# A three-stage transformer kernel on one core: five modulation groups of each feed-forward loop get buffers of their own, with their column sums behind the loop

## The reference, cut to what matters

```python
def ada(cvec, w, b):
    return jnp.split(jax.nn.silu(cvec) @ w + b, 6, axis=-1)

def swiglu(h, w1, w3, w2):
    return (jax.nn.silu(h @ w1) * (h @ w3)) @ w2

x = x + g1 * out_l
x = x + g2 * swiglu(rmsnorm(x, norm2_g[i]) * (1 + sc2) + sh2, ffn_w1[i], ffn_w3[i], ffn_w2[i])
```

## Time and profile before

| what | value |
|---|---|
| median of three runs | 1949.84 us (1944.81 to 1951.23) |
| profiled execution, its own time | 1940.54 us |
| its span, first to last instruction | 1938.7 us |
| busy: TensorE, weight loads, DVE, ACT, POOL | 88%, 56%, 46%, 22%, 19% |
| 40 to 263 us: norm, projections, attention, first residual | TensorE 197.1 of 223 us, clock 0.91 |
| 263 to 479 us: feed-forward loop, layer 0 | TensorE 206.1, DVE 193.7, POOL 103.6 of 216 us, clock 0.97 |
| 479 to 551 us: Fourier mixer | TensorE 62.3 of 72 us |
| 551 to 766 us: feed-forward loop, layer 1 | TensorE 204.3, DVE 194.1, POOL 105.1 of 215 us, clock 0.98 |
| 766 to 940 us: second block's mixer, routing | TensorE 127.4 of 174 us, clock 0.81 |
| 940 to 1938 us: experts | TensorE 882.6 of 998 us, loads at 393 GB/s, DMA share 0.95 |

### The profile page before, as it was taken

The page is one execution under the profiler, slowest core; times in us unless marked ns, Lnnn a source line. Parts: engine busy times, 40 slices in busy tenths (PEclk is TensorE's granted clock), DMA queues, the critical chain, the costliest instruction groups (busy, mean ns, idle before and its releaser), DMA issues.

```text
span 1938.7 us, 24538 instructions
## 1 busy us (share of the span) xinstructions
PE 1704.7 (88%) x9524; PEld 1084.9 (56%) x9524; DVE 888.1 (46%) x1218; ACT 435.8 (22%) x669; POOL 369.1 (19%) x119
## 2 busy tenths in 40 slices
PE   6989889999889998877898798999698999598995
PEld 2863679999689998756543242433242444143432
DVE  5766578998369998675422121221120222021113
ACT  3325543443344443452100000000000000000001
POOL 1631034543334553552000000000000000000000
PEclk9998989999999999887799899999899999899998
DMA  9533367886358886342769999999999999999992
GB/s 356 195 101 117 117 228 272 283 276 206 112 204 276 286 284 211 119 141 78 298 276 421 421 421 421 421 416 421 421 422 421 421 407 421 421 421 421 422 420 107
DMA packets 100463, 586.59 MB, mean 303 GB/s; under 512 B 12208, under 2 KB 13488, under 8 KB 44880
## 3 DMA queue, kind: packets, MB, share of 16 engines
q1 hardware_dynamic: 100368, 585.32, 77.7%
HBM read 584.22 MB, written 1.05 MB: 302 GB/s over the span
## 4 chain that ended last, share of the span: by engine, by line
PE 54%; DMA 19%; DVE 15%; issue 8%; ACT 2%; SPq 1%; DVEq 0%; ACTq 0%
PE psum L990 17%; DMA mraw<-gu_dram 10%; PE psum L1006 10%; DVE acc L1542 5%; DMA araw<-ada_dram 3%; PE psum L966 3%; DMA mraw<-dn_dram 2%; PE psum L566 2%; DMA mlast<-dn_dram 2%; PE psum L567 2%; PE psum L568 2%; PE psum L1019 2%; DVE acc L1541 1%; SPq L378 1%; DVE wl L1814 1%
## 5 line engine op out<-in xcount | busy, mean ns | idle before, releaser
L990 PE MATMUL psum<-mraw,xsat 128*64 128x512 f32 (+2 forms) x1912 | 472.3, 647 | 66.7 <-DMA mraw<-gu_dram 52.6
L1478 POOL TENSOR_TENSOR wl<-raw,wh 128x1024 fp32r<-128x1024 f32 (+1 forms) x100 | 360.1, 3611 | 517.3 <-ACT wh L1106 295.2
L990 PEld LDWEIGHTS psum<-mraw,xsat 128*64 128x64 f32 (+2 forms) x1912 | 160.3, 145 | 353.2 <-issue 352.3
L1006 PE MATMUL psum<-mraw,xsat 128*64 128x512 f32 (+2 forms) x928 | 227.5, 620 | 27.0 <-DMA mlast<-dn_dram 18.9
L747 PE MATMUL psum<-ah,wh 128*128 128x256 f32 x704 | 203.5, 289 | 15.4 <-DVE al L1589 11.6
L748 PE MATMUL psum<-al,wh 128*128 128x256 f32 x704 | 201.4, 286 | 0.0
L749 PE MATMUL psum<-ah,wl 128*128 128x256 f32 x704 | 201.2, 286 | 0.0
L566 PE MATMUL psum<-ah,wh 128*128 128x256 f32 (+1 forms) x440 | 136.6, 311 | 35.0 <-DVE al L1589 11.3
L1006 PEld LDWEIGHTS psum<-mraw,xsat 128*64 128x64 f32 (+2 forms) x928 | 78.3, 141 | 154.6 <-issue 151.7
L747 PEld LDWEIGHTS psum<-ah,wh 128*128 128x128 f32 x704 | 137.2, 195 | 17.0 <-issue 12.0
L2107 DVE TENSOR_TENSOR oacc<-psum,oacc 128x512 f32<-128x512 f32 x64 | 41.2, 685 | 229.1 <-PE psum L1019 229.1
(11 more groups left out here) (341 smaller groups left out, 2457.2 us busy)
## 6 DMA issues: line engine op xcount, KB each, us to landing
mraw<-gu_dram SPq DMA_DIRECT2D x239, 1024.0 KB, 19.3
mraw<-dn_dram SPq DMA_DIRECT2D x116, 1024.0 KB, 24.9
araw<-ada_dram SPq DMA_DIRECT2D x128, 512.0 KB, 4.4
raw<-ffa_dram SPq DMA_DIRECT2D x44, 1024.0 KB, 7.3
raw<-blk_dram SPq DMA_DIRECT2D x56, 512.0 KB, 3.7
raw<-ffb_dram SPq DMA_DIRECT2D x44, 512.0 KB, 5.1
mlast<-gu_dram SPq DMA_DIRECT2D x17, 1024.0 KB, 20.9
mlast<-dn_dram SPq DMA_DIRECT2D x12, 1024.0 KB, 22.4
```

What stands on the lines that cost most here:

```text
L990: last = mm(ps[4 + n][a * w:(a + 1) * w, :], xs[:, k * P + a * w:k * P + (a + 1) * w], slots[slot][:, i * 2 * D + n * 512:i * 2 * D + (n + ...
L1006: last = mm(ps[n][a * w:(a + 1) * w, :], at[:, k * P + a * w:k * P + (a + 1) * w], slots[slot][:, i * D + n * 512:i * D + (n + 1) * 512], ...
L1478: sub = lambda o, a, b: nc.gpsimd.tensor_tensor(o, a, b.bitcast(F32), ALU.subtract)
```

## The change

`acc` stays for the groups outside the loops. Inside a loop each of the five groups has a buffer of its own in `accl` [128 x 5 x 1024] (it lies over `vdft`), addressed by a register that moves with the pass, so that nothing in the loop waits for column sums. The column step leaves the loop. Behind the loop TensorE makes the sums as rows (`loop_rows`): for each half of 512 columns five products with a 128 x 32 matrix of one column of ones, the first four into four strips of 32 rows, the fifth added to the first strip. ACT copies the rows to `lrow`, TensorE turns them into forty columns with eight products (`loop_columns`, behind the norm's sums), and DVE adds forty biases at once (`loop_mods`). DVE's bias of group 5 and 11 moves ahead of the loop. In `norm_split(4)` the gain now follows the reciprocal. POOL's clears wait for the last loop's column products, because `accl` and `lrow` share memory with what is cleared. Two constants are added to `con`, 69 columns in all: `strip` (128 x 64, zero but for column 32) and `pick5` (128 x 5, which picks rows 0, 32, 64, 96 and 1). The hunks of the two constants are left out:

```diff
@@ -188,7 +188,11 @@
...
         tabs = sb("tabs", [P, 2, 3, T], F32, base)
-        vdft = sb("vdft", [P, TT, 4, 2 * T], F32, base)
+        over = ExitStack()
+        vdft = sb("vdft", [P, TT, 4, 2 * T], F32, over)
+        over.close()
+        accl = sb("accl", [P, 5 * AG], F32, base)
+        lrow = sb("lrow", [P, AG], F32, base)
         base.close()
...
@@ -240,7 +244,7 @@
...
         ps = [psum[:, i, :] for i in range(8)]
-        ps45, ps67 = [psum[:, i:i + 2, :].rearrange("p a n -> p (a n)") for i in (4, 6)]
+        ps01, ps45, ps67 = [psum[:, i:i + 2, :].rearrange("p a n -> p (a n)") for i in (0, 4, 6)]
...
@@ -545,6 +549,25 @@
...
+            def loop_rows(l):
+                pe.wait_ge(s_ada, 8 * (9 + 6 * l))
+                for half in range(2):
+                    for i in range(5):
+                        a, one = 32 * (i % 4), _C["strip"] + (32 if i < 4 else 31)
+                        last = mm(ps[half][a:a + 32, :], con[:, one:one + 32],
+                                  accl[:, i * AG + half * 512:i * AG + (half + 1) * 512], start=(i < 4), stop=(i > 0),
+                                  skip_group_check=True)
+                last.then_inc(s_adp, 1)
+
+
+            def loop_columns(l):
+                pe.wait_ge(s_arow, 3 + l)
+                pe.wait_ge(s_mod, 6 + 6 * l)
+                for i in range(8):
+                    last = mm(ps[2][:, 5 * i:5 * i + 5], lrow[:, i * P:(i + 1) * P], C("pick5", 5), start=True, stop=True)
+                last.then_inc(s_acol, 5)
+
+
             def norm_sums(n):
...
@@ -769,21 +792,17 @@
...
                         gate_up(f0 + (2 + u), u)
-                        if u == 2:
-                            pe.wait_ge(s_ada, i * 8 + (8 * (5 + 6 * l)))
-                            pe.wait_ge(s_mod, i + (6 + 6 * l))
-                            for k in range(8):
-                                last = mm(ps[2][:, k:k + 1], acc[:, k * P:(k + 1) * P], ones[:, 0:1], start=True, stop=True)
-                            last.then_inc(s_acol, 1)
                         down(f0 + (1 + u), u + 1)
...
             ffn(0)
+            loop_rows(0)
...
             norm_sums(2)
+            loop_columns(0)
             pe.wait_ge(s_par, DFT_IN)
...
@@ -810,9 +829,11 @@
...
             ffn(1)
+            loop_rows(1)
...
             norm_sums(4)
+            loop_columns(1)
             for b in range(B_2, B_V2):
...
@@ -1118,6 +1139,10 @@
...
+            def loop_row(l):
+                act.wait_ge(s_adp, 9 + l)
+                A(lrow[:, :], ps01, ACT.Copy).then_inc(s_arow, 1)
+
             def norm_root(n, width=T):
...
@@ -1295,6 +1320,7 @@
...
             norm_squares(2, x_by_ffn(0))
+            loop_row(0)
             norm_root(2)
...
@@ -1319,6 +1345,7 @@
...
             norm_squares(4, x_by_ffn(1))
+            loop_row(1)
             act.wait_ge(s_fdn, 1 + 2 * NF)
...
@@ -1504,6 +1531,7 @@
...
             pool.wait_ge(s_fml, 2 * NF)
+            pool.wait_ge(s_acol, 17)
             nc.gpsimd.memset(rga[:, :, :], 0.0).then_inc(s_zero, 1)
...
@@ -1546,7 +1574,7 @@
...
                 if j == 0:
-                    dve.wait_ge(s_acol, g)
+                    dve.wait_ge(s_acol, {11: 6, 17: 12}.get(g, g))
                 else:
...
@@ -1563,6 +1591,14 @@
...
+            def loop_mods(l):
+                g = 6 + 6 * l
+                dve.wait_ge(s_acol, g + 5)
+                TTn(mod[:, 8 * g:8 * g + 40].rearrange("p (g i) -> p g i", i=8),
+                    ps[2][:, 0:40].rearrange("p (i g) -> p g i", g=5),
+                    vec[:, _V["ada_b"] + 8 * g:_V["ada_b"] + 8 * g + 40].rearrange("p (g i) -> p g i", i=8), ALU.add
+                    ).then_inc(s_mod, 5)
+
             def m_col(g, j):
...
@@ -1577,9 +1613,13 @@
...
             def norm_split(n, gain, g_shift, hl):
-                norm_gain(gain, g_shift)
+                if n != 4:
+                    norm_gain(gain, g_shift)
                 dve.wait_ge(s_rt, n + 1)
                 link(V_.reciprocal(rstd[:, 0:T], rt[:, 0:T]))
+                if n == 4:
+                    loop_mods(1)
+                    norm_gain(gain, g_shift)
                 for j in range(DJ + 2):
...
@@ -1606,6 +1646,8 @@
...
                             mod_ready(1)
+                        if n == 2:
+                            loop_mods(0)
                         norm_gain(gain, g_shift)
...
@@ -1813,32 +1855,25 @@
...
+                mod_ready(base_g - 1)
                 down_lo(0, 0)
...
                     loaded = dve.snap(i * 64 + 16 * (base_n // 2 - 7))
-                    col = dve.snap(i * 8 + 8 * (base_g - 1))
-                    cols = dve.snap(i + base_g)
+                    g0 = dve.snap(i * AG)
                     for u in range(4):
                         mul(f0 + u, u % 2)
-                        if u == 0:
-                            dve.wait_ge(s_acol, cols)
-                            TTn(mod[:, bass.ds(col, 8)], ps[2][:, 0:8], vec[:, bass.ds(col + _V["ada_b"], 8)], ALU.add
-                                ).then_inc(s_mod, 1)
                         for j in (2 * u, 2 * u + 1):
                             dve.wait_ge(s_araw[j % 2], loaded + 16 * (j // 2))
-                            if j == 0:
-                                dve.wait_ge(s_acol, cols)
-                            else:
+                            if j > 0:
                                 dve.wait_ge(s_ada, n0 + j)
-                            ada_step(acc[:, :], araw[:, j % 2, :], csil[:, j:j + 1] if l == 0 else V("c2", j), j
+                            ada_step(accl[:, bass.ds(g0, AG)], araw[:, j % 2, :], csil[:, j:j + 1] if l == 0 else V("c2", j), j
                                      ).then_inc(s_ada, 1)
...
                 mul(NF - 2, 0)
-                mod_ready(base_g + 4)
                 mul_lo(NF - 2, 0)
...
```

More of the change, by code:

```diff
@@ L116 @@
 for _name, _m in [("ident", 128), ("ones", 128), ("triu", 128), ("iota", 128), ("iota32", 32), ("pair8", 32), ("head8", 64),
-                  ("bcast8", 8 * QD), ("cos", T), ("sin", T), ("rot", ROPE), ("mask", 2 * P), ("ekey", NEXP), ("capkey", NEXP), ("capval", NEXP), ("erow", 1), ("first", 1), ("pick", 2)]:
+                  ("bcast8", 8 * QD), ("cos", T), ("sin", T), ("rot", ROPE), ("mask", 2 * P), ("ekey", NEXP), ("capkey", NEXP), ("capval", NEXP), ("erow", 1), ("first", 1), ("pick", 2), ("strip", 64), ("pick5", 5)]:
     _C[_name] = _n
@@ L2178, in constants @@
     put("bcast8", np.repeat(np.eye(HEADS), QD, axis=1))
+    put("strip", np.broadcast_to(np.arange(64) == 32, (P, 64)) * 1.0)
+    put("pick5", (r[:, None] == np.array([0, 32, 64, 96, 1])) * 1.0)
     put("pick", np.eye(32, 2)[r[:64] % 32])
```

## The result

Seven runs of the changed kernel gave a median of 1934.49 us (1927.47 to 1938.81), seven runs of the kernel before on the same chip 1944.81 us: ratio **0.9918, 95% interval [0.9896, 0.994]**. The forecast was 8.3 us less, 0.4%; the ratio says 0.8%. (The two medians lie 10.3 us apart, the averages of the same runs, 1947.6 and 1933.0, 14.6.) The direction and the next bound of the loops came as forecast; the size was about half of what the ratio says, for terms that the sum had too small or not at all. The profiled execution took 1928.56 us (span 1926.7), 12.0 less than that of before (1940.54).

The account below looks back on a forecast made before the run. TensorE's column step bounded the loops, with the load chain next at 36.8 us a pass. Loops -13.0, layer 0's tail +1.6, layer 1's +3.0 and constants +0.1 gave -8.3 from 1949.84: 1941.5 us, range 1930 to 1951.

Parts of the forecast that it names:

- The next bound: In the feed-forward loops, what limits a four-tile pass once the column step is gone: 36.8 us a pass, POOL first.
- the load chain: In the loops, wide load, ACT copy, POOL split, DVE accumulate, next wide load's issue: 18.5 us over two tiles.
- The chosen state: In the loops, POOL's split comes first and DVE's accumulate ends behind it, in all passes: 36.8 us a pass.
- The loops, -13.0: Both feed-forward loops: -4.9 and -3.5 us up to the fifth waits, -2.3 twice behind them; ends -32.0 and -7.4.
- Layer 0's tail, +1.6: Behind layer 0's loop: row sums of about 3.6 us put the reciprocal +1.3 later, the 40-column add +0.3.
- Layer 1's tail, +3.0: Behind layer 1's loop: POOL's clears delay its block splits and DVE's norm products; +3.0 us, ends 0.45 and 3.6.
- The start, +0.1: Constants' load: 69 more columns, 35 KB in one load, cost +0.1 us.
- The end, nothing: Expert stage behind the loops: a gain or loss ahead of it passes through in full, with no term of its own.
- TensorE's floor: Rival for the loops: only TensorE remains as bound, passes of 34.56 us, 1922.5 us in all; chance 0.10.
- Accumulate first: Rival for the loops: DVE's accumulate keeps coming before POOL's split, passes of 35.8 us, 1933.5 us; chance 0.16.
- the chain taking all: Rival for the loops: passes of 37.5 us, like the first pass's 9.37 a tile, 1947 us; chance 0.24.
- The slower tails: Rival behind the loops: row sums not side by side take 9.2 us, layers pay 7.2 and 8, 1957 us; chance 0.08.

Follow-up runs that it names:

- early_wide: Changed kernel with SP issuing each wide load between the two chunk loads of the tile before: 1908.51 us, ratio 0.9808.
- half_wide: Changed kernel loading only the first 512 KB of each wide weight tile from the third on (result wrong): 1907.29 us, a single run.
- before_shift: Kernel before with eight unused one-column products placed once between the two loops, so TensorE's later code lies further on: 1943.74 us, a single run.
- before_again: Kernel before, unchanged, profiled a second time: 1950.23 us, a single run.
- wait_columns: Changed kernel with TensorE's old wait and eight one-column products on constants put back into each pass: 1953.74 us, ratio 1.003.
- idle_columns: Changed kernel with eight unused one-column products on constants in each pass, without a wait: 1935.28 us, ratio 0.9941.

## Why the prediction was right and wrong

- **The next bound: right.** 36.8 us a pass by the load chain; measured 36.8 and 36.7 in the first profile, 36.9 and 37.2 in the second. The 18.5 us chain over two tiles named the wide load as its longest piece, and both ways to have it sooner removed the bound. The chosen state was too simple: POOL does not stay first, both orders occur.
- **The page's rule.** The Trainium skill ("DMA: Bandwidth & Descriptors", section "Anatomy of one DMA") has a formula, fitted to loads that GpSimd issues, that gives an estimate of 4.4 us for the wide load; by it loads were no bound at all. Here SP issues the load among others, and its median is 7.3 us in the profiles of before and after, and 6.1 when it is issued earlier. early_wide and half_wide show that the difference decides the pass, so the measured time was rightly taken.
- **The loops, -13.0: the step that failed.** The two first profiles differ by 12.9. But the base was one execution whose ten steps drew a single half-clock stretch (1.7 us lost). The three profiles of before and before_shift lost 1.7, 8.5 and 10.2, on average 6.8, all of which the change takes away. Their loops average 431.7 us for both layers, the changed kernel's two profiles 415.7: **-16.0**. Of these 6.8 are the clock's and 9.2 the wait's and the products'. The forecast had 1.5 of the first without knowing it (the long first pass stood in its 152.1 us) and 11.5 of the second. So the clock gave 5.3 more and the passes, 36.9 on average instead of 36.8, with the rest of the loop 2.3 less; that -13.0 is met by the two first profiles is partly luck. The row was there: the earlier trace rows has 38.96 us from the first to the second step and 37.45 for the other passes, and the prediction asked for no cause of these 1.5 us, nor for the clock behind a step; it looked at the clock behind none of the steps, only in the full stretch. So the cost of a step was put at wait plus products, 2.8 us, and the clock it can cost afterwards was left out.
- **Layer 0's tail, +1.6.** The reciprocal starts 7.75 us behind the loop's end, 6.45 before in the first profile: +1.3, as worked out; it was 5.76 in three others, so +2.0 is the usual. The 40-column add is hidden but for its 0.2 us.
- **Layer 1's tail, +3.0.** DVE is through with the norm 22.7 us behind the loop's end (754.4 to 777.07), where the first profile of before has 20.7 (765.6 to 786.26) and the three others of kernels with the old step 19.5 to 20.0: +2.0 to +3.2, about as worked out. The stages themselves (both tails and all else in them), "between" and "to first expert product" together, are 258.7 us on average of the two profiles of after, and 256.3 on average of before, before_again and before_shift: **+2.3** for the two, where 4.6 stood. Single stages scatter by more than that, so the difference is not assigned to a term.
- **The start, +0.1.** 265.5 and 266.0 against 263.9 to 264.8: +1.4. No run varied the constants, and the profiles of kernels with the same longer load differ among themselves by 2.2 us (264.9 to 267.1), so its cause is open.
- **The end, nothing: the second step that failed, by 3.** The forecast let everything behind the loops pass through unchanged. No reason was given, beyond the stage's being fed by loads. Moving TensorE's code took away a 2 us stop and, with it, 3.4 us at half clock.

Sum of these averages, from few profiles of each kernel: -16.0 + 2.3 + 1.4 - 3.0 = -15.3 us, 0.8% of 1945, which is the ratio measured. The forecast's -8.3 lacks 3.0 in the loops and 3.0 at the end, had 2.3 too much in the tails and 1.3 too little at the start: 3.0 + 3.0 + 2.3 - 1.3 = 7.0.

- **The rivals.** TensorE's floor did not come, but was reached by one moved load: the forecast's end for the loops, -32.0, is what early_wide has against the first profile of before (427.0 to 395.0 us). Accumulate first and the chain taking all are out by the passes of 36.7 to 37.2. That the time of the first of them, 1933.5 us, is nearly the measured one is luck: its passes are 35.8, and neither the clock nor the end is in it. The slower tails are out by the row sums' 3.62 us.

## What to carry to other kernels

A step on the bounding engine that waits for another engine costs its wait, its work, and on TensorE perhaps the clock of the next few microseconds: look at the clock behind each such step, in more than one execution, before pricing its removal. Then ask what the next bound is and whether something cheap moves that too: here two changes worth 14 us (1947.01 to 1932.98) and nothing alone were worth 38 together (1947.01 to 1908.51), because the slower bound hid the other. And a difference in a stretch that the change does not touch should be tried with a shift of the code before it is credited to the change.

## What the runs showed of the hardware

- Half clock comes in stretches of 3 to 7 us behind a wait followed by small products, and not each time: 13 stretches behind 40 such steps in the four profiles with the old step, 5 behind 10 in wait_columns, 2 behind 10 steps with the wait alone, none behind 10 steps with the products alone, where TensorE's waits were at most 0.7 us (idle_columns, 310 to 450 us).
- A shift of TensorE's code by eight unused products shortened the stretch from the first expert product to the end by 3.0 us (991.6 to 988.6): 2.0 a stop in the transposes, the rest in part half clock behind it. The three profiles with the stop have 991.6 to 991.8 us, the nine without it 988.5 to 988.9.
- A 1 MB load took a median of 7.3 us when it was issued behind the narrow load of the tile before, and 6.1 when it was issued between that tile's two chunk loads, at 283 and 303 GB/s of the core's traffic. Cut to 512 KB, in the old place, it took 5.7 (half_wide).
- A product with a single large operand in SBUF can be held as well: DVE's plain product of 128 x 1024 took 4.60 us under POOL's split, and 0.75 at its shortest in the same profile. The multiply that reads a bank took its 0.42 us under another of POOL's splits.
